# One gate product of the merge stage is computed between the first attention unit's scores

## The reference

```
s  = q·k (window of 3 blocks of 128, and the context);  p = exp(s - max);  o = (p·v)/denom
y  = sigmoid(g_rnn)*(y_rnn @ w_o_rnn) + sigmoid(g_attn)*(y_attn @ w_o_attn)
x1 = x + g1 * (y @ w_out)          g_attn = hx @ w_in[:, COL_GB:]
g1, sh2, sc2, g2 = the modulation vectors silu(c) @ w_mod + b_mod
```

## Time and profile before

| | |
|---|---|
| median of 3 runs | 1796.19 us (1795.05 to 1799.88) |
| profiled execution, first to last instruction | 1793.2 us |
| PE busy in it | 1759.5 us, 98% |
| attention stage (PE, first score to last weighing) | about 616.8 to 773 us |
| merge stage (PE, first gate row to last attention row) | 774.0 to 950.6 us |

### The profile page before, as it was taken

One profiled execution on the slowest core, in us unless ns is written; L12 is line 12 of the kernel. 1 busy time (PEld: TensorE's weight loads), 2 busy tenths in 40 slices (PEclk: granted clock), 3 DMA queues, 4 the chain that ended last, 5 costly groups with the idle time before them and its releaser, 6 DMA issues.

```text
span 1793.2 us, 23179 instructions
## 1 busy us (share of the span) xinstructions
PE 1759.5 (98%) x8348; PEld 1467.8 (82%) x8348; DVE 1217.6 (68%) x1377; ACT 716.4 (40%) x918; POOL 551.6 (31%) x261
## 2 busy tenths in 40 slices
PE   7999999999999999999999999999999999999998
PEld 5897888888788789877888878888888888888887
DVE  7978666669516487878217379999989988514425
ACT  5335556566101188840002135444444444302205
POOL 1036666766345476635446710000000000000000
PEclk9999999999999999999999999999999999999999
DMA  9230111111344200057215512222122224523212
GB/s 372 68 112 27 58 60 50 50 50 46 136 149 159 70 1 0 1 178 255 83 58 201 167 43 94 94 82 94 73 82 91 82 84 163 191 97 127 68 36 94
DMA packets 55570, 176.90 MB, mean 99 GB/s; under 512 B 11730, under 2 KB 12114, under 8 KB 54868
## 3 DMA queue, kind: packets, MB, share of 16 engines
q1 hardware_dynamic: 46388, 147.22, 23.2%
q10 hardware_dynamic: 9120, 28.84, 5.0%
HBM read 139.86 MB, written 30.93 MB: 95 GB/s over the span
## 4 chain that ended last, share of the span: by engine, by line
PE 82%; DVE 10%; DMA 4%; issue 2%; ACT 2%; SPq 0%; POOL 0%; ACTq 0%; DVEq 0%; POOLq 0%
PE acc L900 16%; PE acc L901 16%; PE acc L902 16%; PE gp L900 10%; PE gp L901 10%; PE gp L902 10%; DVE wg L2391 2%; PE acc L1196 1%; DMA wg<-in_mod_rest 1%; DVE wgr L2391 1%; DMA wst<-in_w_in 1%; DMA wgr<-in_mod_rest 1%; DVE hx_lo L2254 1%; DVE y_lo L2254 1%; DVE T_lo L2524 0%
## 5 line engine op out<-in xcount | busy, mean ns | idle before, releaser
L900 PE MATMUL acc<-hx_hi,whi_both 128*128 128x512 f32 x672 | 263.0, 391 | 3.4 <-ACT sg L1404 1.5
L901 PE MATMUL acc<-hx_lo,whi_both 128*128 128x512 f32 x672 | 261.9, 390 | 0.0
L902 PE MATMUL acc<-hx_hi,wlo_both 128*128 128x512 f32 x672 | 261.7, 389 | 0.0
L726 POOL TENSOR_TENSOR whi_both<-wst,ones 128x1024 fp32r<-128x1024 f32 x57 | 149.8, 2628 | 258.7 <-PE acc L902 230.2
L728 POOL TENSOR_TENSOR wlo_both<-wst,whi_both 128x1024 fp32r<-128x1024 f32 x57 | 178.3, 3129 | 4.5
L900 PEld LDWEIGHTS acc<-hx_hi,whi_both 128*128 128x128 f32 x672 | 126.2, 188 | 32.9 <-ACT sg L1404 2.7
L902 PEld LDWEIGHTS acc<-hx_hi,wlo_both 128*128 128x128 f32 x672 | 126.2, 188 | 26.6
L901 PEld LDWEIGHTS acc<-hx_lo,whi_both 128*128 128x128 f32 x672 | 126.3, 188 | 25.1
L900 PE MATMUL acc<-T_hi,fac_hi 128*128 128x512 f32 x264 | 102.9, 390 | 0.3 <-DVE fac_lo L2563 0.3
L902 PE MATMUL acc<-T_hi,fac_lo 128*128 128x512 f32 x264 | 102.8, 389 | 0.0
L901 PE MATMUL acc<-T_lo,fac_hi 128*128 128x512 f32 x264 | 102.7, 389 | 0.0
(11 more groups left out here) (385 smaller groups left out, 4647.3 us busy)
## 6 DMA issues: line engine op xcount, KB each, us to landing
wst<-in_w_in SPq DMA_DIRECT2D x43, 512.0 KB, 3.5
wst<-in_w_up SPq DMA_DIRECT2D x26, 512.0 KB, 4.1
wg<-in_mod_rest ACTq DMA_DIRECT2D x24, 512.0 KB, 5.0
ffn_row_scratch<-ca SPq DMA_DIRECT2D x24, 512.0 KB, 2.6
wst<-in_w_down SPq DMA_DIRECT2D x32, 384.0 KB, 3.1
g_in<-ffn_row_scratch SPq DMA_DIRECT2D x24, 512.0 KB, 7.4
wup<-in_w_up SPq DMA_DIRECT2D x22, 512.0 KB, 4.1
wmod<-in_mod_first SPq DMA_DIRECT2D x16, 512.0 KB, 15.3
```

Source lines behind the costliest of these rows:

```text
L726: nc.gpsimd.tensor_tensor(whi[s][:, 0:kc, :], wst[s][:, 0:kc, :], ones_of(kc), mult).then_inc(S["w_hi"], 1)
L900: mm(out_ap, w_h, x_h, start=first, stop=False)
L901: mm(out_ap, w_h, x_l, start=False, stop=False)
L902: return mm(out_ap, w_l, x_h, start=False, stop=last)
```

## The change

The gate row of chunk 0 (GB0) is computed inside the step of the first attention unit: its first half between the scores of the heads 1 and 2, its second half after the scores of head 3, where the 18 small matmuls are taken out. POOL splits its weights right after the first unit's queries. ACT copies the finished row out of `acc[1]` into two tiles (`gb_part`, in memory that the attention needs from its third unit on), SP stores them in device memory (`gb_d`), and when attention is over SP loads them back into `sg[0]`. The merge stage then computes each gate row one step earlier than its attention row: GB1, OA0, GB2, OA1, ..., GB7, OA6, OA7. Gate rows use `acc[0]`, attention rows `acc[1]`, except the last. Every sigmoid on ACT moves one place ahead of the modulation loads: the sigmoid of row 0 (from `sg[0]` to `sg[0]`) and that of row 1 stand where that of row 0 stood, and so on. At the end, six of the `low` instructions go ahead of the merge of chunk 6, and ACT may make the high parts as soon as GB7, the last reader of hx, is done.

```diff
@@ -228,6 +207,7 @@
     pt_lo = sb("pt_lo", B + 80896, [P, NKB, HALF], f32r)
+    gb_part = [sb(f"gb_part{h}", (B + 70656, B + 80896)[h], [P, HALF]) for h in range(2)]
     crow = [sb("crow0", B + 16384, [P, D_MODEL]), sb("crow1", B + 32768, [P, D_MODEL])]
@@ -280,6 +260,7 @@
     ga_d = nc.dram_tensor("ga_scratch", [KC, P, SEQ], f32).ap()
+    gb_d = nc.dram_tensor("gb_scratch", [P, SEQ], f32).ap()
     x1_d = nc.dram_tensor("x1_scratch", [KC, P, SEQ], f32).ap()
@@ -311,7 +292,7 @@
             "fn_loaded": ("ctx_loaded", 16), "x1_loaded": ("late_loaded", 32), "row_copied": ("kw_hi_s", 2), "st_rstd": ("sq_pair", KC - 1), "st_full": ("sq_columns", 1),
-            "st_diag": ("vc_s", 2), "st_spread": ("mask_b", 2), "st_sum": ("k_lo_s", 1),
+            "sg_again": ("q_cos", KC), "st_diag": ("vc_s", 2), "st_spread": ("mask_b", 2), "st_sum": ("k_lo_s", 1),
         }
@@ -568,20 +549,34 @@
                     .then_inc(t1_loaded[s], 16)
-            for s in range(2):
-                load_w(col(w_in, COL_GB, s), W_S4 + 2 * s)
-                load_w(col(w_oa, 0, s), W_S4 + 2 * s + 1)
-                if s == 0:
-                    sp.wait_ge(S["o_read"], N_KV * XT)
-                    for e in range(2):
-                        sp.wait_ge(t1_stored[e], 16 * KC // 2)
-                load_t1(s, s)
-            with sp.Fori(1, KC // 2) as i:
+            load_w(col(w_in, COL_GB, 0), W_S4)
+            load_w(col(w_in, COL_GB, 1), W_S4 + 1)
+            load_w(col(w_oa, 0, 0), W_S4 + 2)
+            slot_read(sp, A_S4)
+            for h in range(2):
+                sp.dma_start(gb_d[:, HALF * h:HALF * (h + 1)], gb_part[h][:, :]).then_inc(ga_stored[h], 16)
+            load_w(col(w_in, COL_GB, 2), W_S4 + 3)
+            sp.wait_ge(S["o_read"], N_KV * XT)
+            for e in range(2):
+                sp.wait_ge(t1_stored[e], 16 * KC // 2)
+                sp.wait_ge(ga_stored[e], 16 * (KC - 1))
+            sp.dma_start(sg[0][:, :], gb_d).then_inc(sg_loaded[0], 16)
+            load_t1(0, 0)
+            load_w(col(w_oa, 0, 1), W_S4 + 4)
+            load_t1(1, 1)
+            with sp.Fori(1, KC // 2 - 1) as i:
                 for s in range(2):
-                    load_w(col(w_in, COL_GB + P * s, 2 * i), W_S4 + 2 * s, per=4, i=i)
-                    load_w(col(w_oa, P * s, 2 * i), W_S4 + 2 * s + 1, per=4, i=i)
+                    load_w(col(w_in, COL_GB + P * (s + 1), 2 * i), W_S4 + 2 * s + 1, per=4, i=i)
+                    load_w(col(w_oa, P * s, 2 * i), W_S4 + 2 * s + 2, per=4, i=i)
                     wait(sp, S["merged"], 2 * i + s - 1)
                     load_t1(2 * i + s, s)
+            load_w(col(w_in, COL_GB, KC - 1), W_S4 + 13)
+            load_w(col(w_oa, 0, KC - 2), W_S4 + 14)
+            sp.wait_ge(S["merged"], KC - 3)
+            load_t1(KC - 2, 0)
+            load_w(col(w_oa, 0, KC - 1), W_S4 + 15)
+            sp.wait_ge(S["merged"], KC - 2)
+            load_t1(KC - 1, 1)
             def load_xres(m, s):
@@ -845,7 +840,7 @@
             def part_of_merge(part):
-                n0, a0 = W_S4 + part // 2, A_Q + 6 + part // 2
+                n0, a0 = W_S4 + 1 + part // 2, A_Q + 7 + part // 2
                 s = n0 % 2
@@ -859,6 +854,8 @@
                 split_queries(n, kh, u)
+                if isinstance(u, int) and u == 0:
+                    split_w(W_S4, last_use=A_Q + 6)
                 if before:
@@ -866,9 +863,10 @@
             units(pool, step, finish)
-            with pool.Fori(0, KC) as i:
-                split_w(W_S4 + 2, last_use=A_S4, per=2, i=i)
+            with pool.Fori(0, KC - 1) as i:
                 split_w(W_S4 + 3, last_use=A_S4 + 1, per=2, i=i)
+                split_w(W_S4 + 4, last_use=A_S4 + 2, per=2, i=i)
+            split_w(W_S4 + 17, last_use=A_S4 + 15)
             def add_square(m):
@@ -1180,6 +1178,8 @@
                 t = block_base(n, u) + j
+                if j == 2 and isinstance(u, int) and u == 0:
+                    slot_read(pe, A_S4)
                 if j == 0 and isinstance(u, int) and u == 0:
@@ -1231,10 +1231,14 @@
                         flip(*before, j)
+                else:
+                    weights(W_S4)
+                    slot_free(A_S4)
+                    half(A_S4, W_S4, 0, hx_hi, hx_lo)
                 score(n, kh, u, 2)
...
                 if not before:
-                    keep_running(acc[0], 18)
+                    half(A_S4, W_S4, 1, hx_hi, hx_lo).then_inc(S["acc_full"], 1)
                 if before:
@@ -1242,11 +1246,12 @@
             pe.wait_ge(S["o_read"], N_KV * XT)
-            product(A_S4, W_S4, hx_hi, hx_lo)
-            product(A_S4 + 1, W_S4 + 1, y_hi, y_lo, paced="z_lo_s")
-            with pe.Fori(1, KC) as i:
-                product(A_S4, W_S4, hx_hi, hx_lo, per=2, i=i)
-                product(A_S4 + 1, W_S4 + 1, y_hi, y_lo, per=2, i=i)
+            product(A_S4 + 1, W_S4 + 1, hx_hi, hx_lo)
+            product(A_S4 + 2, W_S4 + 2, y_hi, y_lo, paced="z_lo_s")
+            with pe.Fori(1, KC - 1) as i:
+                product(A_S4 + 1, W_S4 + 1, hx_hi, hx_lo, per=2, i=i)
+                product(A_S4 + 2, W_S4 + 2, y_hi, y_lo, per=2, i=i)
+            product(A_S4 + 15, W_S4 + 15, y_hi, y_lo)
             weights(W_S5)
@@ -1626,12 +1631,17 @@
                 act_of(r_hi[c][:, :], Y[:, c, :], ACT.Copy).then_inc(S["y_hi_s"], 1)
-            def merge_gate(a0, m, s, before):
-                full(act, a0, 2, m)
-                if before is not None:
-                    act.wait_ge(*before)
-                act_of(sg[s][:, :], acc[1][:, :], ACT.Sigmoid).then_inc(acc_read[1], 1)
+            def merge_gate(m, s, before):
+                full(act, A_S4 - 1, 2, m)
+                act.wait_ge(*before)
+                act_of(sg[s][:, :], acc[0][:, :], ACT.Sigmoid).then_inc(acc_read[0], 1)
+            def first_merge_gate():
+                full(act, A_S4)
+                act.wait_ge(S["q_rope"], N_HEADS)
+                act_of(gb_part[0][:, :], acc[1][:, 0:HALF], ACT.Copy)
+                act_of(gb_part[1][:, :], acc[1][:, HALF:SEQ], ACT.Copy).then_inc(acc_read[1], 1)
             gate_sigmoid(KC - 1, 0)
@@ -1717,6 +1727,9 @@
                     act.wait_ge(S["k_lo_s"], 1)
+                if isinstance(u, int) and u == 2 and j == 0:
+                    for h in range(2):
+                        act.wait_ge(ga_stored[h], 16 * (KC - 1))
                 act_of(pt_hi[:, kb, :], pt_bank(j), ACT.Copy).then_inc(S["pt_hi_s"], 1)
@@ -1753,6 +1766,8 @@
                     out_block(*before)
+                else:
+                    first_merge_gate()
             units(act, attention, lambda n, kh, u: ([high_block(n, kh, u, j) for j in range(NKB)], out_block(n, kh, u)))
@@ -1780,21 +1795,22 @@
                 load_g1(j)
-            merge_gate(A_S4, 0, 0, None)
+            act.wait_ge(sg_loaded[0], 16 * KC // 2)
+            act_of(sg[0][:, :], sg[0][:, :], ACT.Sigmoid).then_inc(S["sg_again"], 1)
+            merge_gate(1, 1, (S["row_silu"], 1))
             for j in range(6, 14):
                 load_g1(j)
-            merge_gate(A_S4, 1, 1, (S["row_silu"], 1))
+            merge_gate(2, 0, (S["merged"], 1))
             for j in range(14, 22):
                 load_g1(j)
-            merge_gate(A_S4, 2, 0, (S["merged"], 1))
+            merge_gate(3, 1, (S["merged"], 2))
             for j in range(22, EARLY_SUMS):
                 load_g1(j)
-            merge_gate(A_S4, 3, 1, (S["merged"], 2))
             with act.Fori(2, KC // 2) as i:
                 for s in range(2):
-                    merge_gate(A_S4, 2 * i + s, s, (S["merged"], 2 * i + s - 1))
-            full(act, A_S4 + 14)
+                    merge_gate(2 * i + s, s, (S["merged"], 2 * i + s - 1))
+            full(act, A_S4 + 13)
             for c in range(KC):
@@ -2377,10 +2393,15 @@
             def merge(m, s, i=0):
-                slot_read(dve, A_S4 + 2 * s, 4, i)
-                full(dve, A_S4 + 2 * s + 1, 4, i)
-                v.tensor_tensor(sg[s][:, :], acc[0][:, :], sg[s][:, :], mult).then_inc(acc_read[0], 1)
-                slot_read(dve, A_S4 + 2 * s + 1, 4, i)
+                last = isinstance(m, int) and m == KC - 1
+                if isinstance(m, int) and m == 0:
+                    dve.wait_ge(S["sg_again"], AT["sg_again"] + 1)
+                else:
+                    slot_read(dve, A_S4 - 1 + 2 * s, 4, i)
+                a0, per, bank = (A_S4 + 15, 0, 0) if last else (A_S4 + 2 + 2 * s, 4, 1)
+                full(dve, a0, per, i)
+                v.tensor_tensor(sg[s][:, :], acc[bank][:, :], sg[s][:, :], mult).then_inc(acc_read[bank], 1)
+                slot_read(dve, a0, per, i)
                 dve.wait_ge(t1_loaded[s], 16 * i + 16)
@@ -2426,10 +2447,10 @@
                     merge(2 * i + s, s, i)
+            for c in range(KC - 2):
+                low(hx_lo, yq, hx_hi, "mg_hi", "mg_lo", c)
             merge(KC - 2, 0, KC // 2 - 1)
-            for c in range(KC - 1):
```

(2 more changed lines are left out.)

## The result

The changed kernel takes 1786.45 us (median of 4 runs, 1783.88 to 1788.14); the kernel before, on the same chip, took 1795.62 us (median of 4). The ratio is 0.9941 with a 95% interval of 0.9929 to 0.9953: 0.5 to 0.7% faster. The forecast was 1787.2 us. The profiled execution has a span of 1784.5 us, forecast 1784.2.

The account below looks back on a forecast made before the run. PE, busy 98% of the span at full clock, was taken to bound the kernel. The terms -10.88 + 2.5 + 0 - 0.6 = -9.0 us took the median from 1796.19 to 1787.2 us, range 1784.0 to 1791.5.

Parts of the forecast that it names:

- The reading of the clock: Whole kernel: PE's granted clock is at full speed, the 2.4 GHz level, in every slice; no size in the sum.
- The moved product: Merge stage: one product row of 48 matmuls leaves it, -10.88 us, provided PE sets the pace there.
- The fill: First attention unit: the moved row exceeds the hole, so unit 1 starts 3.01 us later.
- What is given back: Attention after the first unit: of the 3.01 us lateness 2.5 us stay, bounds 1.9 and 3.0.
- The split beside the rotation: Before the first unit: POOL's weight split may put off two DVE rotation instructions by 2 us; nothing waits.
- The merge stage: Merge stage: second gate product about 1.0 us late, gone by the fourth; net 0, upper bound +1.0, reductions ±2.0 us.
- the slower rival: Merge stage: reductions overlapping splits turn slow, from the fifth further one on; eight give +7, 1803.2 us; chance 0.05.
- The end of the merge: End of merge stage: earlier last merge and loads remove the output projection's 0.59 us wait; -0.6, bounds 0 and -0.6.
- The sum: Whole kernel: all terms together, -9.0 us, for a median of 1787.2 us and a span of 1784.2; chance 0.58.
- rival 1: Fill's 3.0 us not recovered, extra sigmoid's 1.0 us carried through merge stage, projection still waits: -6.9, 1789.3 us; chance 0.16.
- 2: Attention absorbs the delay better (1.9 us) and one merge-stage reduction becomes fast: -11.6, 1784.6 us; chance 0.09.
- 3: Merge stage: reductions set the pace, waits replace the product; three more slow ones leave -3, 1793.2 us; chance 0.12.

Follow-up runs that it names:

- e1: The kernel before without the 18 small matmuls of the first attention unit: 1796.71 us, ratio 0.9997.
- e9: The kernel before, run again unaltered: 1797.29 us, ratio 1.0004.
- e3: The changed kernel with DVE's old order of merges and low parts at the end of the merge stage: 1792.69 us, ratio 0.9976.
- e4: The changed kernel with the 18 small matmuls put back behind the moved row's second half in the first unit: 1790.38 us, ratio 0.9960.
- e8: The changed kernel, run again unaltered: 1787.52 us, ratio 0.9943.
- e10: The changed kernel with both halves of the moved row behind the last score of the first unit: 1789.49 us, ratio 0.9961.
- e12: The changed kernel, run a third time unaltered: 1787.50 us, ratio 0.9946.
- e2: The changed kernel with GB0 computed at the start of the merge stage and the small matmuls back in the first unit: 1794.91 us, ratio 0.9989.
- e6: The changed kernel with all four early gate sigmoids moved up in ACT's order, ahead of modulation loads: 1784.51 us, ratio 0.9930.
- e5: The changed kernel with only the stored gate row's sigmoid moved on ACT ahead of the three loads before it: 1786.99 us, ratio 0.9946.
- e11: The kernel of e6, run again unaltered: 1785.00 us, ratio 0.9935.

## Why the prediction was right, point by point

- **The reading of the clock.** I took the digit 9 in every slice for full speed in every slice. A 9 is 90% or more, and the trace of the kernel before has stretches at the 1.2 GHz level inside such slices: granted clock 0.50 from 159.7 to 166.5 and from 1043.8 to 1047.1. No term of the sum hangs on it, but it hid from me that single executions differ by such stretches (last section).
- **The moved product, -10.88.** C went from 176.59 to 165.93: -10.66. Over all traces with the old merge stage (before, e1, e9) its mean is 176.2, over those with the new one and ACT's order unchanged (after, e3, e4, e8, e10, e12) 165.5. e2, which has all of the change but the move, keeps 16 products and gains only 2 us. Shown.
- **The fill, +3.01.** A went up by 3.06. The end of the rotation, the maxima and the exponentials of unit 0 stayed where they were. Its normalised probabilities, which I had unmoved too, came 0.6 us later (11.57 against 10.94 us from the first score): a small DVE instruction (L2357) took 0.95 us instead of 0.36 beside POOL's split of the next queries. It cost nothing, since DVE waited 1.88 us for PE afterwards. The transposes did not wait for ACT's copies (they follow the score of 633.32 at 633.44), and ACT did not wait for the stores.
- **What is given back, 0.5.** B went down by 0.65. I had DVE late by 2.4 us at the second unit's maxima; it was 2.6 (633.03 less 629.02, less 1.42). The net price, 3.06 - 0.65 = 2.4 us, is the 2.5 of the forecast. e4 and e10 show that this slack is spent: their extra 4.0 and 1.85 us are in A and do not leave B. That DVE's chain sets the pace in units 1 and 2 is read from the traces; none of these runs changed that chain itself.
- **The split beside the rotation, 0.** One instruction was put off by 1.8 us, DVE had 2.3 us left. The Trainium skill, page "SBUF — State Buffer", section "Who interferes with whom", says that the second to start is held until the first is done. Here POOL's instruction ended at 614.76 and DVE's, with its own 1.23 us, at 615.84: the trace agrees to 0.15 us. The other way round, POOL's first instruction started 0.23 us after a DVE instruction of 1.36 us and took 3.38 us instead of 2.39.
- **The merge stage, 0.** Second gate product at 23.68 us from the stage's start, before 22.75: +0.93. No wait at the third. Fourth at 67.84, before 67.64: +0.20. So the net was right against this one trace; by the means above it is +0.2 as well, but single traces of the kernel before differ by 0.9 us in C, and against e9 alone it would be +0.7. The reason was half right. I had the chain of reductions as the limit that takes the lateness up anyway. It was one of two limits that happen to lie within half a microsecond: in e8 the fourth gate product comes at 67.55 with no wait there (and with none in e12), which is the 1.8 us of the second carried through, and e6 shows that neither limit belongs to the reductions themselves, only to where ACT's sigmoids stand among the loads. And e5, which takes the extra sigmoid out of PE's way, gains 0.9 to 1.3 us of C, so the forecast 0 hid about 1 us that could be had. Reductions over 2 us: 11 before, 10 in the changed kernel, 7 to 10 in e1 to e12, so the slower rival's mechanism did not move against the change.
- **The end of the merge, -0.6.** The mis-sized term: D fell by 1.43. I wrote that PE "did not wait" for the last merge, left the low parts out of account and counted only the 0.59 us of the list of waits. The starts of PE in the trace before show two hesitations for the last low parts, at 954.83 and 960.53, which with the slow first step behind each cost 0.27 and 0.19 us, and the wait at 995.42 costs 0.87 us between starts, not 0.59. That is 1.33 of the 1.43; e2 has all of it.
- **The sum.** -9.0 forecast; -9.7 by the four distances, -9.2 by the medians, -8.7 by the spans. The spans hold what the distances leave out: 1.42 us more ahead of the first score and 0.4 less behind D. The 1.42 us are not the change's: they come from a stretch near 486 us in which the granted clock fell in one trace and not in the other (last section).
- **Rivals.** 1 and 2 were the bounds and lie on both sides; 3 and 4 needed more slow reductions, and there were 10 against 11. Of rival 1's three parts one came partly true, the extra sigmoid; the projection's wait went, and 0.65 us of the fill came back.

## What to carry to other kernels

A hole in the work of an engine that is busy 98% of the span is worth what fits into it: move real work of a later stage there, and cut it so that each piece bridges one wait. Of the first 3.1 us beyond the hole 0.65 came back here; after that every further microsecond was paid (e4, e10). When rows come one step earlier than before, look at what the in-order engines have queued ahead of the consumer: e6, which only moves four ACT instructions ahead of loads that wait, takes the last 2.2 us out of the stage, and at 1784.5 and 1785.0 us (ratios 0.9930 and 0.9935) has the lowest medians of these kernels, with an interval that overlaps the changed kernel's. In the list of waits, add to each wait the slow restart behind it: the distance between starts is the price.

## What the runs showed of the hardware

The granted clock of PE fell after gaps, in stretches too short for the slices of the page to show, and cost 0.8 to 3 us each time. In the 5.82 us without work of e1 and in the 2.33 us wait of e3 it went to the 1.2 GHz level, and PE then worked 4.6 and 6.1 us at it. Shorter gaps did it sometimes: behind the two of the first unit (1.6 and 1.8 us, with small matmuls between) it fell in e2 and not in the kernel before or in e9.

One wait is in all fourteen traces, ahead of anything that differs between the kernels: PE waits near 485 us for a weight split. This is where the 1.42 us of the trace after come from, but for 0.2. The stretch behind it, in the kernel before and in the changed kernel:

```profile
486.40:489.80 3.40, 3.40 (x16) 2.80 (x15) 0.00 (x0) 0.00 (x0) 3.32 (x2) 1.00 0.97 320
```

```profile
486.40:489.80 3.40, 3.40 (x10) 2.61 (x9) 0.00 (x0) 0.00 (x0) 3.32 (x2) 0.51 0.93 365
```

Twelve steps from the first matmul behind the wait took 2.86 us before (485.83 to 488.69) and 4.44 after (485.50 to 489.94): 1.6 us. Of the fourteen traces only those of before and e1 kept the clock up there, and they reach the first score at 616.8 and 616.0; eleven in which it fell once, e2 and e9 among them, reach it at 617.7 to 619.1; e12, in which it fell again at 554 to 558 us, at 620.9. So this lateness belongs to the single execution, whatever the kernel. Nor does the length of the wait decide: it was 1.77 us (before) and 2.41 us (e1) where the clock stayed, 1.94 to 2.70 us where it fell.

At the end of attention, behind a wait of 1.27 us and shorter ones, it fell in e8 and not in the two other traces of the changed kernel, and in e11 but not in e6, the same kernel. The stretches of e8 there:

```profile
768.00:772.00 4.00, 2.49 (x9) 1.39 (x9) 3.59 (x10) 2.73 (x8) 1.24 (x2) 1.00 0.00 0
772.00:776.00 4.00, 3.77 (x18) 3.60 (x19) 2.00 (x4) 2.63 (x6) 1.39 (x2) 0.57 0.01 4
776.00:780.00 4.00, 3.31 (x15) 2.44 (x14) 0.85 (x2) 1.67 (x3) 0.00 (x0) 1.00 0.00 0
```

Its B is 0.8 us longer for that. So 0.8 to 1.6 us of one profile against another can be the clock alone. It may be part of what a fill is worth that it leaves fewer gaps to lose the clock in: in none of the ten traces with the moved row did it fall around the first unit, against two of the four without. That fits, but with so few traces it is not shown.
